# Part of the adaLN modulation moved from the projection into the state-space stage, state inputs begun earlier from PSUM, scan states copied first

## The reference, cut to what matters

```python
mod = (jax.nn.silu(c) @ w_ada + b_ada).reshape(bsz, N_MOD, 1, D_MODEL)
shift1, scale1, gate1, shift2, scale2, gate2 = (mod[:, i] for i in range(N_MOD))
h = _layer_norm(x) * (1 + scale1) + shift1
proj = h @ w_in                              # q, k, v, forget logits, u
att = attend(q, k, v, logf)
ssm, h_re, h_im = _s5(u, h0, ...)            # bu = u @ bb; complex scan; y = c @ h + d u; gelu; glu
mix = jnp.concatenate([att, ssm], axis=-1) @ w_o
x = _layer_norm(ALPHA * x + (1 + gate1) * mix, ln1_g, ln1_b)
h2 = _layer_norm(x) * (1 + scale2) + shift2
m = jnp.square(jax.nn.relu(h2 @ w_up)) @ w_down
x = _layer_norm(ALPHA * x + (1 + gate2) * m, ln2_g, ln2_b)
```

## Time and profile before

| | us |
|---|---|
| median of 3 runs | 3298.78 |
| lowest, highest | 3294.81, 3306.61 |
| profiled execution, own time | 3296.45 |
| its span in the trace | 3294.7 |
| PE busy | 3000.0 (91%) |
| DVE busy | 1399.1 (42%) |
| ACT busy | 882.3 (27%) |
| POOL busy | 354.0 (11%) |

### The profile page before, as it was taken

One profiled execution on the slowest core, in us unless ns is written; L12 is line 12 of the kernel. 1 busy time (PEld: TensorE's weight loads), 2 busy tenths in 40 slices (PEclk: granted clock), 3 DMA queues, 4 the chain that ended last, 5 costly groups with the idle time before them and its releaser, 6 DMA issues.

```text
span 3294.7 us, 40818 instructions
## 1 busy us (share of the span) xinstructions
PE 3000.0 (91%) x16401; PEld 2292.3 (70%) x16401; DVE 1399.1 (42%) x2253; ACT 882.3 (27%) x1272; POOL 354.0 (11%) x303
## 2 busy tenths in 40 slices
PE   6899999966578888799699999999999999999997
PEld 2466666644365555588588888888888888888876
DVE  2511212156804433467624434344333444334568
ACT  1311111144124322345422222122222222222224
POOL 1100000036012101012100000000000000000110
PEclk8999999987679999899799999999999999999999
DMA  8766667670158999776322222222222222223352
GB/s 306 236 200 196 195 193 219 199 96 9 38 155 312 367 354 365 290 241 196 96 83 83 78 88 77 90 82 80 82 83 83 84 83 77 90 77 107 98 162 88
DMA packets 249904, 497.62 MB, mean 151 GB/s; under 512 B 48707, under 2 KB 59187, under 8 KB 247979
## 3 DMA queue, kind: packets, MB, share of 16 engines
q1 hardware_dynamic: 239188, 456.38, 43.7%
q0 software_dynamic: 10528, 38.64, 3.9%
HBM read 473.54 MB, written 21.37 MB: 150 GB/s over the span
## 4 chain that ended last, share of the span: by engine, by line
PE 53%; DVE 3%; issue 1%; ACT 1%; DMA 0%; DVEq 0%; ACTq 0%; SPq 0%
PE ps L327 8%; PE ps L328 8%; PE ps L329 8%; PE ps L322 7%; PE ps L323 7%; PE ps L324 7%; PE ps L331 4%; PE ps L332 4%; DMA raw<-in_w_down 0%; DVE xlo L2014 0%; DVE yt L2335 0%; DVE yt L2325 0%; DVE yt L2546 0%; DVE yt L2484 0%; DVE yt L2483 0%
## 5 line engine op out<-in xcount | busy, mean ns | idle before, releaser
L294 DVE TENSOR_TENSOR wlo<-raw,whi 128x1024 fp32r<-128x1024 f32 x361 | 452.1, 1254 | 894.5 <-ACT whi L289 894.3
L289 ACT ACTIVATE whi<-raw 128x1024 fp32r<-128x1024 f32 x361 | 380.9, 1056 | 1167.8 <-PE ps L332 1095.8
L322 PE MATMUL ps<-xhi,whi 128*128 128x512 f32 x1408 | 556.2, 395 | 15.1 <-DVE kT L2699 4.5
L324 PE MATMUL ps<-xhi,wlo 128*128 128x512 f32 x1408 | 550.8, 391 | 0.0
L323 PE MATMUL ps<-xlo,whi 128*128 128x512 f32 x1408 | 550.5, 391 | 0.0
L327 PE MATMUL ps<-whi,rhi 128*128 128x512 f32 x960 | 376.3, 392 | 5.4 <-DVE rsm L2470 3.9
L328 PE MATMUL ps<-whi,rlo 128*128 128x512 f32 x960 | 374.3, 390 | 0.0
L329 PE MATMUL ps<-wlo,rhi 128*128 128x512 f32 x960 | 374.2, 390 | 0.0
L322 PEld LDWEIGHTS ps<-xhi,whi 128*128 128x128 f32 x1408 | 265.8, 189 | 95.6 <-issue 37.4
L324 PEld LDWEIGHTS ps<-xhi,wlo 128*128 128x128 f32 x1408 | 265.8, 189 | 56.4
L323 PEld LDWEIGHTS ps<-xlo,whi 128*128 128x128 f32 x1408 | 266.1, 189 | 53.9
(11 more groups left out here) (517 smaller groups left out, 3585.2 us busy)
## 6 DMA issues: line engine op xcount, KB each, us to landing
adr<-in_w_ada SPq DMA_DIRECT2D x159, 512.0 KB, 5.7
pg<-in_cache_k SPq DMA_DIRECT2D x128, 512.0 KB, 8.0
pg<-in_cache_v SPq DMA_DIRECT2D x128, 512.0 KB, 5.5
raw<-in_w_up SPq DMA_DIRECT2D x128, 512.0 KB, 3.7
raw<-in_w_down SPq DMA_DIRECT2D x128, 512.0 KB, 3.7
raw<-in_w_in SPq DMA_DIRECT2D x64, 512.0 KB, 5.8
raw<-in_w_o SPq DMA_DIRECT2D x49, 512.0 KB, 4.7
raw<-in_w_ada SPq DMA_DIRECT2D x33, 512.0 KB, 7.0
```

The lines of the kernel that those rows point to most:

```text
L289: nc.scalar.activation(whi[gl % NW][:, :, :], rawt(g)[:, :, :], ACT.Copy).then_inc(S("w_hi"), 1)
L294: nc.vector.tensor_tensor(wlo[gl % NW][:, :, :], rawt(g)[:, :, :], whi[gl % NW][:, :, :].bitcast(F32), ALU.subtract).then_inc(S("w_lo"), 1)
L322: nc.tensor.matmul(acc[:, :], hw[:, k2, n], hi[:, k, :], start=st, stop=False)
L324: mm = nc.tensor.matmul(acc[:, :], lw[:, k2, n], hi[:, k, :], start=False, stop=en)
```

## The change

- The modulation chunks are put in another order (`ORD`): gate1, gate2 and shift2 are done in the first 48 slots of the projection; the last 16 slots have none. The four chunks of scale2 (32 groups) are done in the state-space stage by new functions `adw_*`: one group behind each state input from b = 2 on, two behind each table step, two at the end. Their weights go through three buffers, loaded by SP behind `p_done`; the load of a group waits until the group three before it has been used. Mb, which lies in the same place, is loaded only when all groups have been used. The sum over four strips is now a matmul with a constant `selj`, and the bias is added by ACT.
- DVE's state inputs 0 and 1 stand ahead of `p_done`, and inputs 0 to 3 read PR from a copy in PSUM bank 3 (ACT makes it in the last head) and keep their intermediate product in PSUM bank 2.
- POOL computes 8 of Y's 9 columns; ACT copies the first one, which is c itself.
- After the scan the copy into Hd comes ahead of the sample states; ACT's half waits for the imaginary part alone (`hst`). The transposes of the new states follow the first output step. The tables use PSUM banks 6 and 7 in place of 4 and 5.

```diff
+        ORD = list(range(12)) + list(range(20, 24)) + list(range(12, 20))
+        NGP = 48
+        ADA2 = ADA1 + NGP // 4
-            for q in (2 * ph, 2 * ph + 1):
+            for q in (2 * ph, 2 * ph + 1) if x < NGP else ():
...
-                    sh = [P, GH, T + 1, GC]
+                    sh = [P, GH, T, GC]
...
+                        nc.scalar.activation(Y[i][:, :, 0, :], cT, ACT.Copy, scale=(1.0, -1.0)[i])
+                        nc.scalar.activation(cc[:, i], cT, ACT.Copy, scale=(1.0, -1.0)[i]).then_inc(S("cc"), 1)
+                if h == H - 1:
+                    e.wait_ge(S("powers"), 1)
+                    nc.scalar.activation(ps[3][:, :], PR[:, :, :, :].rearrange("p i g t -> p (i g t)"), ACT.Copy).then_inc(
+                        S("prp"), 1)
...
+        def adw_load(e, g):
+            if g >= GW + 3:
+                e.wait_ge(S("ada_used"), ADA1 * NGC + g - 2)
+            e.dma_start(adw[g % 3][:, :, :], ada_src(ORD[ADA1 + g // NGC], g % NGC)).then_inc(
+                S(f"adb_full{g % 3}"), 16)
+        def adw_pe(e, g):
+            p, q = ADA1 + g // NGC, g % NGC
+            if q == 0 and p >= ADA2 + 2:
+                e.wait_ge(S("ada_g"), p - 1)
+            e.wait_ge(S(f"adb_full{g % 3}"), ADB0[g % 3] + 16 * (g // 3) + 16)
+            for k2 in range(GK):
+                k = q * GK + k2
+                j = k % 4
+                mm = nc.tensor.matmul(ps[4 + p % 2][32 * j:32 * j + 32, :], scT[:, k, :], adw[g % 3][:, k2, :],
+                                      start=k < 4, stop=k >= KC - 4)
+            mm.then_inc(S("ada_used"), 1)
...
                 inputs(b)
+                if b >= 2:
+                    adw_pe(e, GW + b - 2)
+                if b in X_TURN:
+                    adw_turn(e, X_TURN[b])
...
+                adw_pe(e, GK0 + 2 * b)
+                adw_pe(e, GK0 + 2 * b + 1)
...
+            side = b < XP
+            tab = ps[3][:, :].rearrange("p (i g t) -> p i g t", i=2, g=GP) if side else PR
+            mid = [ps[2][:, i * 256:i * 256 + 256].rearrange("p (q t c) -> p q t c", q=2, t=T) if side else
+                   (xtmp, xtmp2)[i][:, :, :, :] for i in (0, 1)]
...
-            nc.vector.tensor_tensor(xtmp[:, :, :, :], pi, bi, ALU.mult)
+            nc.vector.tensor_tensor(mid[0], pi, bi, ALU.mult)
...
             p_done(e)
-            for b in range(NX):
+            for b in range(2, NX):
                 x_part(e, own, b)
```

More of the change, by code:

```diff
@@ L589, in ada_slot @@
             n, ph = ADA1 + x // 4, x % 4
-            if ph == 0 and n >= ADA1 + 2:
+            if ph == 0 and ADA1 + 2 <= n < ADA2:
                 e.wait_ge(S("ada_g"), n - 1)
@@ L923, in program @@
         U = at("U", [P, G, NJ], W0 + 55296)
-        Xn = [at(f"Xn{i}", [P, 2, 2, T, GC], W0 + (73728, 108544)[i]) for i in range(2)]
+        Xn = [at(f"Xn{i}", [P, 2, 2, T, GC], W0 + (73728, 94208)[i]) for i in range(2)]
         XT = [at(f"XT{i}", [P, 4, P], W0 + 87552 + 2048 * i) for i in range(2)]
@@ L952, in program @@
         zr = at("zr", [P, 8, T, NJ], R0 + 16384)
-        NX = GP // 2
+        XP = 4
         GLN = T * NJ // 2
+        adw = [at(f"adw{i}", [P, GK, CW], R0 + 33280 + 4096 * i) for i in range(3)]
+        gparw = [at(f"gparw{i}", [P, CW], pos[0] + 2048 * i) for i in range(2)]
+        assert pos[0] + 4096 <= W0
+        selj = at("selj", [P, 32], FIN0)
+        GW = 2 * NGP
+        GK0 = GW + NX - 2
+        GR = GK0 + 16
+        X_PART = {10: ADA2}
+        X_TURN = {12: ADA2}
+        X_MOD = {13: ADA2}
@@ new lines, in adw_turn, with adw_part @@
+        def adw_turn(e, p):
+            e.wait_ge(S("ada_g"), p + 1)
+            e.wait_ge(S("ada_m"), p)
+            if p == ADA2:
+                e.wait_ge(S("selj"), B("selj") + 1)
+            for b in range(4):
+                mm = nc.tensor.matmul(ps[3][:, 16 * b:16 * b + 9], gparw[p % 2][:, b * P:b * P + P], selj[:, 0:9],
+                                      start=True, stop=True)
+            mm.then_inc(S("ada_t"), 1)
+        def adw_part(e, p):
+            e.wait_ge(S("ada_used"), NGC * (p + 1))
+            nc.scalar.activation(gparw[p % 2][:, :], ps[4 + p % 2][:, :], ACT.Copy).then_inc(S("ada_g"), 1)
@@ L956, in p_done, with adw_mod @@
+        def adw_mod(e, p):
+            e.wait_ge(S("ada_t"), p + 1)
+            for b in range(4):
+                x = 4 * ORD[p] + b
+                ins = nc.scalar.activation(modT[:, x, :], ps[3][:, 16 * b:16 * b + 9], ACT.Identity,
+                                           bias=badaT[:, x:x + 1])
+            ins.then_inc(S("ada_m"), 1)
         def p_done(e):
@@ L968, in s_sp @@
             p_done(e)
+            for g in range(GW, GW + 3):
+                adw_load(e, g)
             for i, n in enumerate(["state_ssm_re", "state_ssm_im"]):
@@ L972, in s_sp @@
                         "b (gp r) n -> (b gp) (r n)", r=2)).then_inc(S("prm_in"), 16)
+            for g in range(GW + 3, GW + 8):
+                adw_load(e, g)
             e.wait_ge(S("zt"), 1)
@@ L975, in s_sp @@
                         zt[:, :, :]).then_inc(S("k_out"), 16)
+            for g in range(GW + 8, NGC * (ADA - ADA1)):
+                adw_load(e, g)
             e.wait_ge(S("K_ev"), 8)
@@ L1284, in s_dve @@
             own = owns["dve"]
+            V = nc.vector
+            V.tensor_reduce(selj[:, :], ident[:, :].rearrange("p (j i) -> p i j", j=4), AX.X, ALU.add).then_inc(
+                S("selj"), 1)
+            e.wait_ge(S("bb"), 1)
+            e.wait_ge(S("prp"), B("prp") + 1)
+            x_part(e, own, 0)
+            e.wait_ge(S("p_acc"), H - 1)
+            x_part(e, own, 1)
             p_done(e)
-            V = nc.vector
-            e.wait_ge(S("bb"), 1)
-            e.wait_ge(S("powers"), 1)
-            for b in range(NX):
+            for b in range(2, NX):
                 x_part(e, own, b)
@@ L2597, in _ @@
                     gate_dma(e, ada_events(x - 4))
-            for x in range(NGP - 4, NGP):
-                if ada_events(x):
-                    gate_dma(e, ada_events(x))
-            for ev in ADA_END:
-                gate_dma(e, ev)
             p_sp(e)
@@ L2886, in _ @@
                     split_dve(e, g, g)
-            for ev in ADA_END:
-                ada_evac(e, own, ev)
             p_dve(e)
```

123 lines of the change are left out of this document (73 added, 50 removed).

## The result

The changed kernel takes 3262.49 us, the median of four runs (3256.28 to 3265.22); its ratio to the kernel before is 0.9883, 95% interval [0.9866, 0.9899]. Forecast were 3266, with 3255 to 3283 as range. Two further sets of runs gave 3261.14 (0.9872 [0.9852, 0.9892]) and 3263.24 (0.9895 [0.9877, 0.9912]). The profiled execution took 3264.54 us, its span is 3262.8.

A forecast was written before the change was run, and what follows sets the result against it. PE was taken to bound the projection, DVE's serial scan the stretch before the state outputs. 17.0 + 2.5 - 0.6 + 13.1 = 32.0 us off the 3298.78 median gave 3266.8, stated as 3266, range 3255 to 3283.

The forecast's parts named there:

- Projection: End of the projection: 16 of 64 slots lose their modulation matmuls; 17.0 us gained, range 15 to 18.
- Behind the projection: From its last matmul to the token loads: sample-sum copy starts at once, no gate store in the way; 2.5 us gained.
- Attention: One of ACT's two copies into Y's first column precedes the first value matmul: 0.6 us lost, range 0 to 1.2.
- State inputs: State-space stage: PE steps of 2.45 us with one modulation group each; the state copy comes 8.9 us earlier.
- Table steps: Behind the state copy: eight pairs of groups add 9.6 us; the table store ends 37.2 us after the copy.
- Scan and outputs: Scan loop ends 42.61 us after the state copy, outputs 12.6 us later; 13.1 us gained by the whole state stage.
- Rival E: State inputs: DVE waits for POOL despite PSUM operands; state copy 2.5 us later, 3268 us; chance 0.06.
- A: State inputs: PE loses its clock in half the steps, 4.3 us instead of 2.45; +13 us, 3279; chance 0.18.
- B: Table steps: the load ring is late, 5.8 us a step, table store 8 us behind the scan; 3274; chance 0.10.
- C: Inputs and tables: PE stays at 1.2 GHz, making the kernel slower than before; 3314 us; chance 0.04.
- D: Projection: the removed slots were free because PE would wait for weights; 17 us less gain, 3283; chance 0.03.

The follow-up runs named there:

- 2: Against the changed kernel: state inputs 0 to 3 read the powers and keep their temporaries in SBUF instead of PSUM; 3264.66 us, 0.9891 of the kernel before.
- 4: Against the changed kernel: POOL forms all nine columns of Y again, without ACT's two copies; 3268.99 us, 0.9907 of the kernel before.
- run 7: Against the changed kernel: six of each eight moved modulation groups left out, with all their loads but the first three; 3256.47 us, 0.9856 of the kernel before.
- run 1: Against the changed kernel: only the modulation's move undone, all 64 projection slots and gate rows back; 3277.99 us, 0.9937 of the kernel before.
- copy early: Against the changed kernel: old state's transposes and copy ahead of the last input step, two groups moved behind the table steps; 3254.87 us, second time 3257.24.

## Why the prediction was right, point by point

- **Projection, 17.0 us.** With all slots its last matmul is at 660.7 in the mean of three profiles, with 48 slots at 642.7 in the mean of eleven (639.3 to 646.9): 18.0. Right, at the upper end of 15 to 18. The stretch that lost its matmuls, from the 48th slot's groups to the last matmul, went from 129.8 us to 108.1 to 112.6, 19.6 less in the mean; the 48th slot comes 1.6 us later.
- **Behind the projection, 2.5 us.** Measured 3.8 in the mean (16.4 to 16.6 us to the token transposes with all slots, 12.5 to 12.7 with 48), where 2.5 was taken: mis-sized. That it meets the bound of 3.8 is luck. The bound priced the sample store by a landing of 3.7 us; it took 2.36 to the token loads, which thus gained 5.3 us, and the slower token load, which was not counted, gave 1.3 back.
- **Attention, -0.6 us.** 105.3 (twice) against 104.1 and 104.4, so 0.9 to 1.2 longer; other kernels with the same attention needed 104.6. Right within the spread of these; the third profile's 110.7 is the other length of the attention, told at the end.
- **State inputs, 8.9 us.** Measured 10.2 (51.9 to 41.7), just under the 10.5 of a step at 2.33 us. The step was 2.22, not the 2.45 of the forecast, and one step at the lower clock took 2 of the 3 us that this won. Nor was it 2.65, the estimate with the row's 0.3 us for one change of mode more. The Trainium skill (TensorEngine Tiling (Array Packing), "Key Properties") says that a change of tiling mode drains TensorE. In this trace, with three shapes in a step, nothing shows beyond what the parts take alone, 0.56, 0.72 and 1.05 us; what of a drain lies inside these no run tells. (The row's 0.3 us was mostly no idle time: the narrow matmuls start 0.32 us behind the last full one, where 0.23 is the usual step.) That DVE does not wait for POOL with an operand in PSUM, and that Y's end holds the rest, was right (2 and 4). But there is little more to win from Y: when it ended 5.7 us nearer to the attention's end, in the third profile, the stage gained 0.6; PE then waited 1.04 us for one of DVE's parts, and one step (3.71 us) again had the lower clock.
- **Table steps, 37.2 us to the store's end.** Measured 40.9 (802.87 to 843.76), 3.7 too little: mis-sized. The steps up to the store's issue grew by 11.8 us (23.6 to 35.4) where 9.6 was counted for the groups, and the store landed in 5.5 us instead of 4.0 (in 4.1 again in run 7, with most of the groups' loads left out). The loads of the tables waited for that landing, not for the last groups, which PE had finished at 842.98. The scan's loop ended 42.55 us behind the copy, as forecast (42.61), so that the whole 3.7 us came out of the cover of DVE's wait: 1.66 us, not 5.4. It held, narrowly, and run 7 shows that the tables were not the bound.
- **Scan and outputs, 13.1 us with the inputs.** From the old state's copy to the outputs 5.5 us less; forecast were 5.6. Behind the outputs 1.0 to 3.6 came back, where 1.4 was counted; that stretch took 66.7 to 67.0 us in five profiles with the new order and 68.7 to 69.4 in six, and why was not tried.
- **Rival E was right as a mechanism to look for, wrong in price.** I put SBUF operands at 2.5 us, PE being "nearly as late anyway"; they are worth 7.3. That step took the parts for delayed until POOL's end only; but none of them is finished then, where four are with PSUM operands, DVE ends 8.5 us later, and PE gains back 1.2 of it.
- **Rivals A to D.** A happened in one step (4.35 us, the 4.3 that I had priced), not in seven. B happened in part: the loads held up PE's weight loading for 7.7 us in eight places, seven of them in the table steps, and PE itself for 2.1 us in three; the scan covered it. C did not occur: inputs and tables ran at 0.90 and 1.00, and only the outputs at 0.50, as before. D fell with run 1.

The terms as measured, 18.0 + 3.8 - 1.0 + 10.2 + 5.5 - 1.0 to 3.6, make 33 to 35.5 us (with the shorter attention); the three ratios, of 3298.78, say 34.6 to 42.2. The forecast of 32 was a little short, by the store behind the projection, the step and the slots. That the two first profiles differ by just 31.9 is chance: their untouched decode stretches differ by 5.5. The range was wider than its reasons: the bounds named for 3255 (10.5, 3.8 and 18) take 1.6, 1.3 and 1.0 us off 3266, which is 3262, and that is where the medians lie (3261 to 3263).

## What to carry to other kernels

Work moved from an engine that bounds one stage into a stage where it waits for another is nearly free (4 of some 22 us here), as long as the stage's own chain is longer than what is put beside it. The store or load that the chain waits for has to be priced beside the traffic that the change adds: of 5.4 us of cover counted here 1.66 were left. Ask of several measures which wait each of them shortens: those on the same wait don't add. When a change is worth a few us in milliseconds, read the length of its stages in several profiles rather than the whole time: stages that it does not touch moved by 8 us.

## What the runs showed of the hardware

DVE's all-SBUF multiply of 256 elements took 1.41 to 4.71 us while POOL's elementwise work ran, each ending 0.28 us behind one of POOL's operations, and 0.42 us with one operand in PSUM beside the same POOL work. The Trainium skill (SBUF — State Buffer, "SBUF: two separate sides") has the port pair that both engines share as a lock held for a whole instruction, which an operation of DVE with two SBUF inputs needs while POOL reads SBUF; the ends of these rows agree.

The attention has two lengths in the same kernel: 104.1 to 105.4 us in eleven profiles and 109.8 to 110.7 in three (the changed kernel's third, slots back, and copy early the second time). Both profiles of the kernel before are of the short kind; whether the change makes the long kind more frequent, two profiles can't say. Windows of the third profile of the changed kernel, and then of its first, in the columns of the earlier trace rows:

```profile
720.00:730.00 10.00, 9.31 (x23) 5.31 (x21) 1.48 (x5) 4.92 (x12) 9.84 (x4) 0.52 0.00 1
730.00:740.00 10.00, 9.22 (x19) 4.33 (x18) 2.20 (x8) 5.14 (x14) 9.92 (x3) 0.50 0.00 0
740.00:750.00 10.00, 9.01 (x34) 5.25 (x33) 3.52 (x12) 6.03 (x17) 9.84 (x4) 0.95 0.00 0
```

```profile
716.00:726.00 10.00, 5.35 (x16) 3.01 (x16) 5.55 (x30) 5.27 (x16) 7.27 (x2) 0.78 0.00 2
726.00:736.00 10.00, 9.01 (x31) 5.10 (x30) 3.52 (x12) 5.20 (x16) 9.84 (x4) 0.88 0.00 0
```

PE waits some 3.9 us for ACT in both ahead of the same values; in the one the granted clock then stays at 0.50, which is 1.2 GHz, for some 20 us with PE busy, in the other it is back at a mean of 0.88 in the second window. In all three long ones the clock is at 0.50 for 20.5 us there, in the eleven others for 6.8 to 10.2. Why one and why the other was not tried. Of the 5.4 us, the state inputs gave next to nothing back (41.1 against 41.7), though Y was ready 5.7 us nearer to the attention's end.
